# Where the three steps of a 192-token expert chunk stand among the 64-token chunks of a mixture-of-experts stage

## The reference, cut to what matters

```python
top_v, top_i = lax.top_k(logits, TOP_K)
wts = jax.nn.softmax(top_v, axis=-1)
comb = jnp.einsum('tk,tke->te', wts, jax.nn.one_hot(top_i, N_EXPERTS, dtype=f32))
for e in range(N_EXPERTS):
    he = jax.nn.silu(xt @ w_gate[e]) * (xt @ w_up[e])
    y = y + comb[:, e:e + 1] * (he @ w_down[e])
```

## Time and profile before

| | us |
|---|---|
| median of three runs (1590.49 to 1591.68) | 1591.39 |
| the profiled execution | 1587.45 |
| its span, first to last instruction | 1585.6 |
| TensorE busy in the span | 1424.9 (90%) |
| VectorE busy | 654.5 (41%) |
| ScalarE busy | 530.5 (33%) |
| bytes moved by DMA | 497.17 MB |

### The profile page before, as it was taken

One profiled execution on the slowest core, in us unless ns is written; L12 is line 12 of the kernel. 1 busy time (PEld: TensorE's weight loads), 2 busy tenths in 40 slices (PEclk: granted clock), 3 DMA queues, 4 the chain that ended last, 5 costly groups with the idle time before them and its releaser, 6 DMA issues.

```text
span 1585.6 us, 22731 instructions
## 1 busy us (share of the span) xinstructions
PE 1424.9 (90%) x9485; PEld 1016.1 (64%) x9485; DVE 654.5 (41%) x991; ACT 530.5 (33%) x848; POOL 110.0 (7%) x221
## 2 busy tenths in 40 slices
PE   6898789999978789887779999999999999999993
PEld 3786679998867579663358865555555545465552
DVE  2545554548547695410069931312222222222123
ACT  2731454530335655410068821211221121122113
POOL 1014200000002120060000000000000000000001
PEclk9897899999989879979989999999999999999997
DMA  8762564453645339459999989999999999999994
GB/s 351 290 269 106 180 248 169 160 180 113 238 186 213 150 119 384 159 187 423 416 389 421 401 326 422 421 420 421 422 420 421 421 421 421 419 420 422 417 415 164
DMA packets 65085, 497.17 MB, mean 314 GB/s; under 512 B 7537, under 2 KB 7808, under 8 KB 13777
## 3 DMA queue, kind: packets, MB, share of 16 engines
q1 hardware_dynamic: 59202, 473.27, 73.8%
q0 software_dynamic: 5232, 21.20, 3.6%
q10 hardware_dynamic: 542, 1.20, 0.2%
HBM read 477.27 MB, written 18.39 MB: 313 GB/s over the span
## 4 chain that ended last, share of the span: by engine, by line
PE 42%; DMA 18%; DVE 3%; ACT 1%; issue 1%; SPq 0%; POOL 0%; DVEq 0%; ACTq 0%; POOLq 0%
PE bank L2280 40%; DMA ring<-in_expert_rows_dram 12%; DMA hT<-in_expert_rows_dram 5%; PE bank L2860 0%; DVE hT L2091 0%; DMA fT<-y_rows,row_i 0%; DVE hT L2097 0%; DVE arena L2261 0%; ACT plain_lo L1382 0%; PE bank L2891 0%; PE bank L2737 0%; PE bank L2805 0%; PE bank L2889 0%; DVE arena L2253 0%; ACT arena L1492 0%
## 5 line engine op out<-in xcount | busy, mean ns | idle before, releaser
L2280 PE MATMUL bank<-ring,fT 128*64 128x256 f32 (+1 forms) x3352 | 467.5, 427 | 46.9 <-DMA ring<-in_expert_rows_dram 41.6
L2280 PEld LDWEIGHTS bank<-ring,fT 128*64 128x64 f32 x3352 | 232.4, 137 | 259.9 <-issue 106.1
L2280 PE MATMUL bank<-parts,w_hi 128*128 128x264 f32 x1600 | 309.0, 294 | 24.6 <-DVE parts L1667 24.6
L2280 PEld LDWEIGHTS bank<-parts,w_hi 128*128 128x128 f32 x1600 | 258.3, 197 | 35.6 <-issue 23.0
L2280 PE MATMUL bank<-parts,w_lo 128*128 128x264 f32 x800 | 232.4, 291 | 0.0
L2280 PE MATMUL bank<-w_hi,parts 128*128 128x512 f32 x672 | 203.4, 398 | 9.4 <-DVE w_lo L620 9.4
L569 DVE TENSOR_TENSOR w_lo<-ring,w_hi 128x2048 fp32r<-128x2048 f32 x50 | 114.9, 2302 | 140.7 <-ACT w_hi L563 140.6
L2280 PEld LDWEIGHTS bank<-parts,w_lo 128*128 128x128 f32 x800 | 156.4, 196 | 0.0
L2280 PEld LDWEIGHTS bank<-w_hi,parts 128*128 128x128 f32 x672 | 125.2, 190 | 46.4 <-issue 18.0
L1556 ACT ACTIVATE sq<-bank 128x256 f32<-128x256 f32 x42 | 16.1, 384 | 380.1 <-PE bank L2280 380.1
L2280 PE MATMUL bank<-w_lo,parts 128*128 128x512 f32 x336 | 122.8, 393 | 0.0
(11 more groups left out here) (490 smaller groups left out, 1310.9 us busy)
## 6 DMA issues: line engine op xcount, KB each, us to landing
ring<-in_expert_rows_dram SPq DMA_DIRECT2D x288, 1024.0 KB, 12.1
ring<-in_dense_rows_dram SPq DMA_DIRECT2D x48, 2048.0 KB, 8.3
hT<-in_expert_rows_dram SPq DMA_DIRECT2D x48, 1024.0 KB, 12.0
ring<-in_dense_rows_dram SPq DMA_DIRECT2D x8, 1408.0 KB, 6.1
x_rows<-arena POOLq DMA_DIRECT2D x1, 5632.0 KB, 35.1
y_rows<-arena POOLq DMA_DIRECT2D x1, 2560.0 KB, 42.7
ring<-in_dense_rows_dram SPq DMA_DIRECT2D x2, 1024.0 KB, 5.1
arena<-x_rows SPq DMA_DIRECT2D x4, 512.0 KB, 16.9
```

The costliest lines, as they stand in the source:

```text
L2280: return pe.matmul(out, lhsT, rhs, start=start, stop=stop, skip_group_check=True)
```

## The change

The `while` loop behind each small chunk places the pieces of the big job in whole chunks: the bound is a multiple of three, and it grows by three when `(n + 2) * 7 // 32` does (n is the number of the small chunk, from 0 to 34). `big_turn` is put into the list right behind `big_up`. The older insertion behind the next gate stays in the code and finds nothing to do, as no list ends in `big_up` any more.

```diff
@@ -160,7 +160,9 @@
         if _k + 1 < HALF_JOBS:
             MIX.append(("x", _k + 2, 0))
         MIX += [("turn", _k + 1, _c), ("down", _k + 1, _c)]
-    while _placed < min(len(BIG_PIECES), len(BIG_PIECES) * _n // BIG_OVER):
+    while _placed < min(len(BIG_PIECES), 3 * ((_n + 2) * NCHK // BIG_OVER)):
+        if MIX[-1][0] == "big_up":
+            MIX.append(("big_turn", None, MIX[-1][2]))
         MIX.append((BIG_PIECES[_placed][0], None, BIG_PIECES[_placed][1]))
         _placed += 1
```

## The result

The changed kernel took 1665.55 us (median of 4 runs, 1664.25 to 1667.20), the kernel before 1590.94 in the same comparison. The ratio is 1.047, 95% interval 1.0456 to 1.0485: slower by 4.7%, some 75 us. Forecast were 1646 (+55), with a range to 1661. The direction and what bounds the kernel held, the size did not.

A forecast was written before the change was run, and what follows sets the result against it. The weight stream through the seven-half ring was taken as the bound; late halves (6.8 + 0.2 + 0.5 = 7.5 us) plus 0.3 for refilling gave 7.8 us per chunk, 7 x 7.8 = 55 us, so 1646 us, range 1632 to 1661.

The forecast's parts named there:

- What bounds the kernel: In MIX the never interrupted weight stream sets the end: 252 halves x 2.49 us = 627 us, through a seven-half ring.
- The new waits: TensorE ahead of big_up, big_turn and big_down: 1.0 + 1.1 + 1.7 = 3.8 us per chunk, 27 in all.
- the splits are covered: Splits of up and down, queued on ScalarE and VectorE, are ready before TensorE needs them: cost nothing.
- TensorE: gate 0 to 10.1, up from 11.1 to 20.3 ... down from 24.0 to 33.2: TensorE's timetable in us through a run of three big pieces, from the landing of its first half; sets the reload times.
- half 11: Counted from 0 at a run's first half; its reload was forecast to land at 34.2, not 27.4: 6.8 us lost.
- Half 14 is in pace again ... I add 0.3: Behind each run, the refilled queue returns to pace by half 14; its slow restart adds 0.3 us per chunk.
- the dry part: Late landings of halves 11, 12 and 13 in each run: 6.8, 0.2 and 0.5, sum 7.5 us.
- Is the loss recovered: Between runs, DMAs cannot catch up and TensorE waits for data again: all seven runs pay, 7 x 7.8 = 55 us.
- Rival A: In MIX, the ring and TensorE's 31 us of idle time absorb the new waits: no change, 1591 us; chance 4%.
- Rival B: Restarting the queue costs more and splits come late: 9.7 to 10.5 us per chunk, 1659 to 1665; chance 17%.
- Rival C: The new waits are partly covered, half 11 up to 2 us earlier: 5.5 us per chunk, 1630; chance 12%.
- Rival D: TensorE becomes the bound between runs if small chunks exceed 12.2 us: 1650 to 1656; chance 5%.

The follow-up runs named there:

- experiment 1: The changed kernel with useless products put ahead of TensorE's three new waits: 1658.03 us, ratio 1.0406 to the kernel before.
- experiment 4: The kernel before, with at most two loads in the queue: 1653.51 us, ratio 1.0367; with at most three: 1597.62 us, ratio 1.0034.
- filled kernel: The kernel of experiment 1: the changed kernel with useless products ahead of the three new waits, 1658.03 us, ratio 1.0406.
- experiment 2: The changed kernel with six slots for halves in the ring in place of seven: 1686.84 us, ratio 1.0585 to the kernel before.
- turn_at_once: The kernel before with only big_turn moved right behind big_up, big pieces still spread one at a time: 1591.95 us, ratio 1.0002.
- run_of_two: The kernel before with only big_gate and big_up put together, big_turn and big_down one small chunk later: 1616.38 us, ratio 1.0144.

## Why the prediction was wrong

- **What bounds the kernel** (the weight stream, the ring as a closed loop): right. 77.6 of the 80 us are in `MIX`, as DMA time lost in seven dips.
- **The new waits**, 1.0 + 1.1 + 1.7: right to a tenth of a us, all seven times. That the splits are covered: right as well, the fp32r products of `big_down` start at the end of its pairs.
- **The step that failed first**: "TensorE: gate 0 to 10.1, up from 11.1 to 20.3 ... down from 24.0 to 33.2". All these durations came from rows at PEclk 1.00, and I carried that clock over, although the change adds three pauses of TensorE, 3.8 us together, within 14 us. The clock's fall was in neither the sum nor a rival. In five runs of seven the clock fell, and half 11 came 1.6 us later, in the last 3. Priced at 0, measured at some 10 us (experiment 1).
- **The second**: "Half 14 is in pace again ... I add 0.3", the term for the refilled queue. I had seen two slow second landings in the earlier trace rows and took them for a cost of the restart, paid once. It is a cost that goes on while the queue is shallow, mostly as one late load in eight (experiment 4), and some 10 to 12 loads a run are issued to such a queue. The filled kernel has 68 / 7 = 9.7 us a run, of which the dry part that I had worked out is 7.5. That leaves 2.2 where I had 0.3, so 13 us over seven runs; the depth of two or three loads by itself has 0.23 and 0.02 us a load. The landings of the filled kernel say the same apart from any sum: over the pace of 2.49, the landing of half 11 is 49 us late in the seven runs together (forecast 7 x 6.8 = 48), and the 13 landings behind each are 23 us late (forecast 7 x 1.0 = 7).
- The sum mended: 7 x 7.8 = 55, 10 for the clock, 13 for the shallow queue, together 78 of the 80. The 13 are what the filled kernel leaves over, so that the sum comes out says nothing more of them. With only one of the two steps wrong, the time would have been inside the range.
- **Is the loss recovered**: right that not. All seven runs paid, the last one too, and the most (13.4).
- **Rival A** (idle time of TensorE evens it out): refuted by experiment 2, and the other way round by turn_at_once, where the ring does even a wait out. **Rival B** (1659 to 1665) had the measured size at its upper end, and one of its two reasons: restarting does cost more, but the splits were never late. The clock made up the difference, so that the size agrees is partly luck. **Rival C**: no. **Rival D**: no, TensorE waits for data again ahead of every run.
- **The range** took in a worst case of the restart and left out the upper end of B.

Not settled: how a packet of the kind instruction holds up a load in a shallow queue, which is read from coinciding times alone, and why the clock held in the first and the fifth run, with the same three waits.

## What to carry to other kernels

Where a prefetch ring is the bound, cost a new order by the time at which each slot comes back, not by idle shares: seven waits of 1.1 us cost nothing where they stood alone, and with 26 us of waits in a row of heavy pieces 75 us were lost. Price a queue that holds fewer than three loads above the pace of a full one (here 383 GB/s with two, 419 with three). And where a change adds several pauses of 1 us or more close together to a TensorE that ran at the full clock, put the lower clock behind them into the range. One pause of 1.0 or 1.1 us a chunk (run_of_two, turn_at_once) left it at 1.00 here.

## What the runs showed of the hardware that I had not expected

- Three pauses of 1.0, 1.1 and 1.7 us within 14 us, on a TensorE that is busy otherwise, were followed by 3.4 or 6.8 us at 1.2 GHz in five of seven cases (with six slots, in three of seven); useless products in the pauses kept 2.4 GHz in all of them.
- 1 MB loads with never more than two in the queue moved 383 GB/s, with three 419, with up to seven 420.
- The seven loads of the changed kernel that found the queue empty within `MIX` took 4.6 to 4.9 us, those of the filled one 4.6 to 5.0.
- With at most two 1 MB loads in the queue, 26 of 27 packets of the kind instruction (16 KB, some 1 us) fell into a load that landed late; with three loads, 30 such packets stood beside one late landing.
